# Rows of the last five expert blocks kept in SBUF and added by one-hot products, output gate gathered per block, small steps of the dense part reordered

## What is computed

```python
def trunk_layer(x, c, ...):
    mod = silu(c) @ w_ada + b_ada
    sh1, sc1, g1, sh2, sc2, g2 = split(mod, 6)
    h = x * (1 + sc1) + sh1
    z = h @ w_in + b_in                      # a_glu, q, k, v, qi, ki, wi, uv, gates
    y_a = conformer_conv(...); y_b = attend(...); y_c, v_chunk = chunk_sgu(...)
    merged = g_a*(y_a @ w_pa) + g_b*(y_b @ w_pb) + g_c*(y_c @ w_pc)
    x = layer_norm(ALPHA*x + (1 + g1)*(merged @ w_o), ln1)
    h2 = x*(1 + sc2) + sh2
    x = layer_norm(ALPHA*x + (1 + g2)*moe(h2), ln2)

def moe(h, ...):      # 1 of 4 groups, then its two best experts, weights sum to 1
    for e in range(16):
        y += gate[..., e] * ((silu(h @ w_e_gate[e]) * (h @ w_e_up[e])) @ w_e_down[e])
```

## Time and profile before

| | |
|---|---|
| median of three executions | 1105.62 us |
| profiled execution | 1110.89 us |
| its span, first to last instruction | 1109.0 us |
| PE busy | 1009.2 us, 91% |
| DVE, POOL, ACT busy | 492.8, 253.0, 186.2 us |
| mean granted PE clock | 0.948 of full |
| dense part, to the first gather of h2 | 754 us |
| expert blocks, first hidden product to last down product | 761.7 to 1063.7 us |
| end, after the last product | 45 us |

### The profile page before, as it was taken

The page is one execution under the profiler, slowest core; times in us unless marked ns, Lnnn a source line. Parts: engine busy times, 40 slices in busy tenths (PEclk is TensorE's granted clock), DMA queues, the critical chain, the costliest instruction groups (busy, mean ns, idle before and its releaser), DMA issues. The chain is left out here.

```text
span 1109.0 us, 22156 instructions
## 1 busy us (share of the span) xinstructions
PE 1009.2 (91%) x8966; PEld 676.4 (61%) x8966; DVE 492.8 (44%) x1281; ACT 186.2 (17%) x441; POOL 253.0 (23%) x287
## 2 busy tenths in 40 slices
PE   4999999998999999999999999987999999998930
PEld 3777777455876766667777764565655555554510
DVE  2122999972356888855104004677133011010117
ACT  2110112113122212221111110111111111111103
POOL 0000005445121113222325430000221221211133
PEclk8998999999798999999999999986999999999975
DMA  9955645452515206114081317142969899999856
GB/s 307 300 112 157 181 153 204 142 194 78 196 29 162 67 15 193 31 46 113 11 211 36 114 52 300 66 180 96 367 252 417 324 377 392 421 414 419 323 155 121
DMA packets 93733, 214.23 MB, mean 193 GB/s; under 512 B 23465, under 2 KB 48304, under 8 KB 89534
## 3 DMA queue, kind: packets, MB, share of 16 engines
q1 hardware_dynamic: 78388, 186.20, 47.0%
q0 software_dynamic: 6400, 19.01, 5.8%
q10 hardware_dynamic: 8849, 7.64, 2.5%
HBM read 200.46 MB, written 16.92 MB: 196 GB/s over the span
## 5 line engine op out<-in xcount | busy, mean ns | idle before, releaser
L1747 PE MATMUL bank<-arena 128*128 128x288 f32 (+6 forms) x1778 | 444.1, 406 | 6.5 <-issue 2.1
L1747 PEld LDWEIGHTS bank<-arena 128*128 128x128 f32 (+2 forms) x1778 | 321.3, 193 | 121.3 <-issue 45.9
L2138 PE MATMUL bank<-arena 128*32 128x256 f32 x3136 | 181.4, 382 | 8.5 <-issue 6.6
L2138 PEld LDWEIGHTS bank<-arena 128*32 128x32 f32 x3136 | 103.5, 109 | 78.4 <-issue 12.4
L1699 DVE TENSOR_TENSOR arena<-arena,bank 128x128 f32<-128x128 f32 x49 | 14.2, 289 | 229.5 <-ACT arena L1142 229.3
L914 POOL DMA_INDIRECT expert_rows<-arena,ints x49 | 47.7, 974 | 228.0 <-ACT arena L1153 228.0
L864 POOL TENSOR_SCALAR arena<-arena 128x288 f32<-128x288 f32 x48 | 45.3, 943 | 219.5 <-ACT arena L1104 219.5
L2157 PE MATMUL bank<-arena 128*32 128x256 f32 x1568 | 94.6, 381 | 0.0
L1215 DVE SCALAR_TENSOR_TENSOR arena<-arena 128x512 f32<-128x512 f32 x120 | 81.9, 741 | 0.0
L1761 PE MATMUL bank<-arena 128*128 128x288 f32 x256 | 69.2, 428 | 2.6 <-DVEq L1233 2.6
L1751 PE MATMUL bank<-arena 128*128 128x128 f32 (+7 forms) x315 | 51.7, 300 | 17.8 <-DMA arena<-constants 5.0
(11 more groups left out here) (282 smaller groups left out, 880.5 us busy)
## 6 DMA issues: line engine op xcount, KB each, us to landing
arena<-in_w_e_gate SPq DMA_DIRECT2D x16, 2048.0 KB, 11.0
arena<-in_w_e_up SPq DMA_DIRECT2D x16, 2048.0 KB, 16.3
arena<-in_w_e_down SPq DMA_DIRECT2D x16, 2048.0 KB, 21.4
arena<-in_w_ada SPq DMA_DIRECT2D x8, 2048.0 KB, 10.5
arena<-in_w_in SPq DMA_DIRECT2D x8, 2048.0 KB, 10.1
arena<-in_w_ada SPq DMA_DIRECT2D x8, 1024.0 KB, 11.6
arena<-in_x_prompt SPq DMA_DIRECT2D x8, 512.0 KB, 5.2
arena<-in_w_in SPq DMA_DIRECT2D x14, 256.0 KB, 8.2
```

The lines of the kernel that those rows point to most:

```text
L1747: last = pe.matmul(out, a, b, start=k == 0, stop=k == len(pairs_) - 1)
L2138: last = pe.matmul(out, HG[:, g % 2, k, a:a + BLK], gate_up[i % 2][:, :, k, c * P:c * P + P], start=k == 0, stop=k == KT - 1)
```

## The change

Two groups of edits.

**The experts' end.** The results of blocks 44 to 48 (the last two turns, `SENT` = 44, `KEPT` = 5) are not scattered but stay in SBUF. For each of them DVE makes a 0/1 matrix of its slots against the 640 token places (`kept_hot`), and after the last block PE multiplies it with the block's results into PSUM, 20 products of 32 rows x 128 x 256 per token tile, each quarter of a row in its own bank. Every block's result is copied out by DVE instead of ACT, and is there multiplied by the token's weight and by 1 + g2; for that POOL gathers, two blocks ahead, the right quarter row of `mod` for each of the 128 partitions (`gate_rows`, 128 x 256 from DRAM, an indirect DMA per block, two buffers). All other rows are summed in the residual X1 itself: POOL adds first and second choices of the five tiles by ten accumulating DMAs (`firsts`, `seconds`), from block 45 on. Since `expert_rows` now has places that nothing writes, and a second tensor `further_rows` takes the further tiles, both are filled with zeros (2 x 5.24 MB) by two DMAs from POOL at `("ada", 8)`. The expert's end no longer multiplies by 1 + g2; DVE and (with further tiles) PE wait there for `further_added`, which POOL signals after its last accumulating DMA is issued and its branches on `nov` are passed. The slot list carries the index of the token's conditioning row as well, so that `list_up`, `spread` and `spread_up` have a few more small operations.

**The dense part.** Four steps of `plan` around the layer norm of the convolution branch change places, `("proj", "B", 0, 0)` comes after `("gate", "B", 0, 1)`, the last two pairs are merged by DVE (two operations straight from PSUM) instead of by ACT and POOL, and ACT instead of DVE copies the transposed cached keys. The pieces `ada` 10 and 11 get their 1 added by POOL there.

```diff
+SENT = FIRST[NE - 2]
+KEPT = NBLK - SENT
...
-    plan += [("nat", "u", 0), ("nat", "u", 1), ("lnA1", 0), ("ada", 9), ("nat", "u", 2), ("lnA1", 1), ("lnA2", 0), ("nat", "u", 3), ("ada", 10)]
-    plan += [("lnA1", 2), ("lnA2", 1), ("nat", "u", 4), ("mix", 0), ("ada", 11), ("lnA1", 3), ("lnA2", 2), ("mix", 1), ("lnA1", 4), ("lnA2", 3)]
-    plan += [("mix", 2), ("lnA2", 4), ("yc", 0), ("mix", 3), ("yc", 1), ("yc", 2)]
+    plan += [("nat", "u", 0), ("nat", "u", 1), ("lnA1", 0), ("ada", 9), ("nat", "u", 2), ("lnA1", 1), ("nat", "u", 3), ("lnA2", 0), ("ada", 10)]
+    plan += [("lnA1", 2), ("lnA2", 1), ("nat", "u", 4), ("mix", 0), ("ada", 11), ("lnA1", 3), ("lnA2", 2), ("mix", 1), ("mix", 2), ("lnA1", 4), ("lnA2", 3)]
+    plan += [("yc", 0), ("mix", 3), ("lnA2", 4), ("yc", 1), ("yc", 2)]
...
+    plan += [("gate", "B", 0, 0), ("pv", "s"), ("gate", "B", 0, 1), ("proj", "B", 0, 0), ("proj", "B", 0, 1)]
+    for f in range(1, KT):
         for h in range(2):
-            plan += [("gate", "B", f, h)] + ([("pv", "s")] if (f, h) == (0, 0) else []) + [("proj", "B", f, h)]
+            plan += [("gate", "B", f, h), ("proj", "B", f, h)]
...
+                if n == 8:
+                    own.link(pool.memset(ZERO, 0.0))
+                    for rows in (y_d, y2_d):
+                        pool.dma_start(rows[0:2 * SLEN].rearrange("(p n) (h d) -> p (n h) d", p=P, d=512),
+                                       ZERO.unsqueeze(1).broadcast_to([P, 2 * SLEN * 2 // P, 512])).then_inc(ev("zeroed"), 16)
...
+                if n >= 10:
+
+                    own.link(pool.tensor_scalar(bada_buf(n), bada_buf(n), 1.0, None, ALU.add))
...
+        gates = mod_d.rearrange("r (k f) -> (r k) f", f=256)
+
+        def gate_rows(d):
+
+            pool.indirect_dma_start(G2B[:, d % 2, :], None, gates, bass.IndirectOffsetOnAxis(ints[:, I_ROW + d:I_ROW + d + 1], 0)).then_inc(ev(f"g2_in{d % 2}"), 16)
+
+        def add_rows(t, second, src, sem_name):
+            a = t * P + SLEN * second
+            pool.dma_start(X1[0:rows_of(t), t, :], src[a:a + rows_of(t), :], accum_op=ALU.add).then_inc(ev(sem_name), 16)
+
+        def firsts(t):
+            add_rows(t, 0, y_d, f"pair_in{t}")
+
+        def seconds(t):
+            pool.wait_ge(ev(f"pair_in{t}"), 16)
+            add_rows(t, 1, y_d, f"pair_in{t}")
+
+        pool.wait_ge(ev("weights_up"), 1)
+        gate_rows(0)
+        gate_rows(1)
+        for d in range(NBLK - 2):
+
             for g in range(2, TILES):
                 if d == max(4 * g - 10, 1):
                     gather(g)
-
             pool.wait_ge(ev("yo_up"), d + 1)
-            pool.indirect_dma_start(quarters, bass.IndirectOffsetOnAxis(ints[:, I_DEST + d:I_DEST + d + 1], 0), YR[:, d % YRS, :], None).then_inc(stored(d)[0], 16)
+            if d < SENT:
+
+                pool.indirect_dma_start(quarters, bass.IndirectOffsetOnAxis(ints[:, I_DEST + d:I_DEST + d + 1], 0), YR[:, yr_of(d), :], None).then_inc(stored(d)[0], 16)
+            gate_rows(d + 2)
+            if d == SENT + 1:
+
+                for done_ in stored_by(SENT):
+                    pool.wait_ge(*done_)
+                firsts(0)
+                firsts(1)
+                seconds(0)
+        firsts(2)
+        seconds(1)
+        firsts(3)
+        seconds(2)
+        firsts(4)
+        seconds(3)
+        seconds(4)
...
+        for s in range(NOV):
+            with pool.If(nov > s):
+                pool.wait_ge(*far_stored(s // 2 + 1, s % 2))
+        with pool.If(nov > 0):
+            for t in range(NT):
+                for second in range(2):
+                    pool.wait_ge(ev(f"pair_in{t}"), 16 * (second + 2))
+                    add_rows(t, second, y2_d, f"pair_in{t}")
+                pool.wait_ge(ev(f"pair_in{t}"), 64)
+        pool.sem_inc(ev("further_added"), 1)
...
-            d = b - 2
-            if d >= 0:
-                act.wait_ge(ev("dn_full"), d + 1)
-                if d >= YRS:
-                    act.wait_ge(*stored(d - YRS))
-                if d == 0:
-                    act.wait_ge(ev("weights_up"), 1)
-                act.activation(YR[:, d % YRS, :], banks[6 + d % 2][:, 0:256], ACT.Copy, scale=WBLK[:, d:d + 1]).then_inc(ev("yo_up"), 1)
...
+            elif kind == "proj" and pair_no[key[1:]] >= len(pairs) - 2:
+
+                _, x, f, h = key
+                n = pair_no[key[1:]]
+                cols, pj = slice(h * HALF, h * HALF + HALF), PJ[:, n % 2, :]
+                dve.wait_ge(*mm.taken(("gate", x, f, h)))
+                dve.wait_ge(*mm.full(key))
+
+                dve.wait_ge(ev("merged"), n)
+                stt(pj, GT[:, n % 2, :], 1.0, mm.tile(key)[:, 0:HALF], ALU.add, ALU.mult).then_inc(mm.free(key), 1)
+                dve.wait_ge(*mm.taken(key))
+                tt_(MG[:, f, cols], MG[:, f, cols], pj, ALU.add).then_inc(ev("merged"), 1)
...
+        def result_up(d):
+
+            dve.wait_ge(ev("dn_full"), d + 1)
+            if YRS <= d < SENT:
+                dve.wait_ge(*stored(d - YRS))
+            dve.wait_ge(ev(f"g2_in{d % 2}"), 16 * (d // 2 + 1))
+            stt(YR[:, yr_of(d), :], banks[6 + d % 2][:, 0:256], WBLK[:, d:d + 1], G2B[:, d % 2, :], ALU.mult, ALU.mult).then_inc(ev("yo_up"), 1)
...
+        def kept_hot(k):
+            link(tt_(OHT[k], KOFF[:, k, :].unsqueeze(2).broadcast_to([P, NT, TS]), RCON[:, R_LO:].unsqueeze(1).broadcast_to([P, NT, TS]), ALU.is_equal))
...
-                if b == NBLK - 6:
-                    done(dve.memset(EPSN, EPS))
-                    dve.wait_ge(ev("rows2_in"), 64)
-                    done(ts(BC2[:, 0, :], BC2[:, 0, :], 1.0, None, ALU.add))
-                    link(ts(BC2[0:NS, 1, :], BC2[0:NS, 1, :], 1.0, None, ALU.add))
+                if b == 20:
+                    link(dve.memset(EPSN, EPS))
+                    kept_tokens()
+                if 21 <= b < 21 + KEPT:
+                    kept_hot(b - 21)
...
+        dve.wait_ge(ev("further_added"), 1)
+        dve.wait_ge(ev("rows2_in"), 32)
         for t in range(NT):
-            n, a, m = rows_of(t), GAT[0:rows_of(t), t, :], TOTAL[0:rows_of(t), t:t + 1]
-            dve.wait_ge(ev(f"pair_in{t}"), 16)
-            link(tt_(a, a, BC2[0:n, 0 if t < 4 else 1, :], ALU.mult))
-            link(dve.tensor_tensor_reduce(out=a, in0=a, in1=X1[0:n, t, :], scale=1.0, scalar=0.0, op0=ALU.add, op1=ALU.add, accum_out=m))
-            ts(NMEAN[0:n, t:t + 1], m, -1.0 / (32 * D), None, ALU.mult).then_inc(ev("row_mean"), 1)
-            link(ts(m, m, -1.0 / D, None, ALU.mult))
-            stt(OUT[0:n, t, :], a, m, BC2[0:n, 2, :], ALU.add, ALU.mult).then_inc(ev("less_mean"), 1)
+            n = rows_of(t)
+            x, sums, total = X1[0:n, t, :], sum_banks(t), TOTAL[0:n, t:t + 1]
+            dve.wait_ge(ev(f"pair_in{t}"), 32)
+            dve.wait_ge(ev("rows_summed"), t + 1)
+            by_quarter = x.rearrange("p (c f) -> p c f", c=4)
+            link(dve.tensor_tensor_reduce(out=by_quarter, in0=by_quarter, in1=sums[0:n], scale=1.0, scalar=0.0, op0=ALU.add, op1=ALU.add, accum_out=total))
+            ts(NMEAN[0:n, t:t + 1], total, -1.0 / (32 * D), None, ALU.mult).then_inc(ev("row_mean"), 1)
+            link(ts(total, total, -1.0 / D, None, ALU.mult))
+            stt(OUT[0:n, t, :], x, total, BC2[0:n, 0, :], ALU.add, ALU.mult).then_inc(ev("less_mean"), 1)
...
+        pe.wait_ge(ev("he_ready"), NBLK)
+        pe.wait_ge(ev("het_up"), NBLK)
+        for t in range(NT):
+            n = rows_of(t)
+            if t == 1:
+                pe.wait_ge(ev("yo_up"), NBLK)
+            if t >= 2:
+                pe.wait_ge(ev("row_mean"), t - 1)
+            for k in range(KEPT):
+                if t == 0:
+                    pe.wait_ge(ev("yo_up"), SENT + k + 1)
+                for c in range(4):
+                    rows = slice(BLK * c, BLK * c + BLK)
+                    last = pe.matmul(sum_banks(t)[0:n, c, :], OHT[k][rows, t, 0:n], YR[rows, YRS + k, :],
+                                     start=k == 0, stop=k == KEPT - 1)
+            last.then_inc(ev("rows_summed"), 1)
```

172 lines of the change are left out of this document (97 added, 75 removed).

## The result

| | before | after |
|---|---|---|
| median of four executions | 1104.76 us | 1129.16 us (1125.85 to 1132.00) |
| ratio, 95% interval | | 1.021, 1.018 to 1.024 |
| profiled execution, its span | 1110.89, 1109.0 us | 1132.00, 1129.8 us |
| first hidden product of the experts | 761.7 us | 776.4 us |
| from there to the end of the last down product | 302.0 us | 310.3 us |

The span grew by 20.8 us: 14.7 in the dense part, 8.3 in the expert loop, −2.2 at the end. 1128 us was forecast.

The account below looks back on a forecast made before the run. PE, busy 91% of the span, was taken to bound the kernel, so edits pay where it waits or in the last 45 us. Terms 19 − 2.5 + 6 + 0 = +22.5 on 1105.6 gave 1128 us, overall range 1108 to 1145.

Parts of the forecast that it names:

- Fills, +19: Dense part: piece 8's write queues behind the zero fills, so PE stands before the lnA1 3 transposes; +19 us (8 to 30).
- Dense order, −2.5: Dense part: reordered steps and last merges on DVE shorten waits at w_o and pv; −2.5 us (−4 to 0).
- Gate rows, +6 (2 to 14): Expert blocks: 49 gathers of 128 KB compete with weight loads where DMA is full; +6 us (2 to 14).
- PE meets it as later weights at the start of turns: Expert turns, 868 to 1012 us: gathers delay weights, raising PE's waits there from 6.9 to about 13 us.
- End, 0: After the last blocks: DVE starts 6 us later, then saves 6.2 us without the 1 + g2 multiply; 0 (−5 to +5).
- The fill does not bite: Rival, dense part: q0's later DMAs land beside the fills, so part 1 falls away; +3.5, 1109 us; chance 0.10.
- faster: Rival, whole kernel: fills through by about 263.5 us, gathers free, POOL signals before 1079.16; 1095 us; chance 0.08.
- The gate rows bind: Rival, expert blocks: gathers taking 10 us or more delay DVE's copy-out and PE; +26, 1154 us; chance 0.08.
- The chain: Expert blocks: DVE copy-out, POOL's scatter and gather issues, landing; 9.5 against 11.2 us per two blocks, so hidden.
- The row sums don't overlap: Rival, end: PE's 32-row products run one after another, 5.6 us a tile; +9 to +15, 1140 us; chance 0.05.

Follow-up runs that it names:

- the first job: The changed kernel's first timing beside the kernel before, one execution profiled: 1129.16 us, ratio 1.021.
- the second job: The changed kernel again, unchanged, timed beside the kernel before and in one job with three variants of it: 1138.7 us, ratio 1.029.
- The early signal: Against the changed kernel, POOL signals further_added right after its first three accumulating DMAs when there are no further tiles: 1130.2 us, ratio 1.024.

## Why the prediction held, step by step

**Fills, +19: right in mechanism, place and size, with part of the working off.** The second landing was at 283.5 us (288 taken, 275 to 296 as ends), the stand 19.42 us (21 us of lateness forecast), and the transposes were 17.5 us late. The price of q1, 2.8 us per MB, was about right: alone the fills took 2.6. The forecast called the DMA engines idle up to 272.9 us, but the earlier trace rows show that only from 264 on. SP's loads held q0 back until 252, some 4 us, and met the second fill again from 276 on. The forecast allowed 9 us for a meeting at the end alone, so the landing came 4.5 us early. From the landing to the transposes it took 6.7 us, not 5.7. The Trainium skill's fit ("DMA: Bandwidth & Descriptors", "Anatomy of one DMA — SWDGE (gpsimd) path"), as an estimate, has both landed by about 275 us and the first after 14. The first took 18.4, of which 3.8 passed while q1 held the engines; the trace disagrees with the fit for the pair, which moved at 378 GB/s and not 436 even when alone (9.06 MB in 24 us). The measurement decides.

What the forecast did not say is that +19 is the price in this kernel and not the fill's own: it is 11 us on the kernel before. The stand ends 33 to 35 us after the first issue, so what brings PE there earlier is lost in it.

**Dense order, −2.5: right alone, but the two terms don't add.** Alone it gives 3 to 4 us with an interval of 0.4 to 6. With the fills in place it gives nothing: the kernel before with the fills is at 1.011, with fills and dense edits at 1.015. Together the two cost 14.3 us (1121.0 against 1106.6), where the forecast had 19 − 2.5 = 16.5. The sum held because its first term was worked out from the place in this kernel and not from the fills alone.

**Gate rows, +6 (2 to 14): the term that was mis-sized.** The loop grew by 8.3 us in the first job, of which 2.7 lie in the first three blocks and come without gathers as well. In the second job it grew by 13 (315.3 against 302.0), and the gathers' own price there is 15.1, above the range's end. The step that failed is "PE meets it as later weights at the start of turns": these waits were forecast to rise from 6.9 to about 13 and were 10.3, then 7.8. The rest is PE's clock behind longer waits and, in all later jobs, stops and a slower pace inside the blocks, which no row of before shows. The range's upper end, 14, takes in the second job's 13 by luck, since it stood for slower packets.

**End, 0: right in both halves.** DVE began 22.2 us after the last down product (1108.93 − 1086.7), where before it was 15.5, so 6.8 us later than before, by the landing, the branches and the signal, +6 in the forecast; from its first operation to its last it took 6.2 us less, as forecast. The other 2.7 us of the −2.2 lie behind DVE's last operation, which the forecast did not touch; no experiment here was made for that part. The early signal shows that the 6.8 were for taking: −6.6.

**The rivals.** "The fill does not bite" and "faster" fell with ACT's wait of 22.11 us. "The gate rows bind": the prediction named DVE waiting for `g2_in` in the expert blocks as a sign of being wrong, and that sign came, 30.5 us in 11 blocks. The chain was not hidden from DVE as forecast, but with one gather per block no wait of PE came of it; the two blocks of lead were enough. "The row sums don't overlap": 40 recorded products of a tile take 2.8 to 3.1 us (8.34 / 3, 6.25 / 2), about DVE's 2.73 per tile, and two tiles are done ahead, so they don't bind.

That 1128 came out as 1129 owes something to the job: 1138.7 in the other, still in the range.
